# Retention by blocks with a carried state, and four picking rounds moved into the sparse attention

## What is computed

```python
def retention(q, k, v, gate):          # chunks of C = 128 tokens, N = 4 chunks
    scores = einsum('bnchd,bnmhd->bnhcm', qf, kf) * decay_in      # inside a chunk
    inner = einsum('bnhcm,bnmhd->bnchd', scores, vf)
    chunk_state = einsum('bnmhk,hm,bnmhv->bnhkv', kf, zeta, vf)   # K^T V of a chunk
    # scan over chunks: R <- chunk_decay * R + state, prev = R before the chunk
    cross = einsum('bnchk,bnhkv,hc->bnchv', qf, prev, xi)
    o = (inner + cross)
    o = o * rsqrt(mean(o * o, axis=-1) + EPS)                     # per token and head
    return o * silu(gate)

def dsa_attention(q, k, v, qi, ki, wi):  # per block of 128 queries
    iscore = sum_h relu(qi . ki) * wi, causal
    _, sel = top_k(iscore, 128)
    p = softmax(q . k[sel] * d ** -0.5);  out = p @ v[sel]
```

## Time and profile before

| | us |
|---|---|
| median of 3 runs (2241.92 to 2244.69) | 2242.39 |
| the profiled execution | 2242.63 |
| its span on the core | 2240.7 |
| PE busy | 2124.0 (95%) |
| DVE busy | 1257.8 (56%) |
| ACT busy | 806.5 (36%) |
| POOL busy | 78.9 (4%) |

### The profile page before, as it was taken

The page is one execution under the profiler, slowest core; times in us unless marked ns, Lnnn a source line. Parts: engine busy times, 40 slices in busy tenths (PEclk is TensorE's granted clock), DMA queues, the critical chain, the costliest instruction groups (busy, mean ns, idle before and its releaser), DMA issues.

```text
span 2240.7 us, 28429 instructions
## 1 busy us (share of the span) xinstructions
PE 2124.0 (95%) x10880; PEld 1735.8 (77%) x10880; DVE 1257.8 (56%) x2223; ACT 806.5 (36%) x1468; POOL 78.9 (4%) x89
## 2 busy tenths in 40 slices
PE   6998898999999899999999999989879999999998
PEld 5786576888888688887788888778856677888887
DVE  4588447778654424683654545575776746322334
ACT  3333544333423435213422222243446644222222
POOL 0003200000000010000000000001001100000000
PEclk9999798999999899999999999999989999999999
DMA  5221123656442232101355545512400013433221
GB/s 189 89 84 38 38 76 106 204 169 207 132 169 94 74 105 89 44 1 57 123 182 193 176 162 170 169 62 66 151 2 2 2 57 113 132 94 94 94 99 53
DMA packets 146835, 233.10 MB, mean 104 GB/s; under 512 B 7341, under 2 KB 83725, under 8 KB 146445
## 3 DMA queue, kind: packets, MB, share of 16 engines
q1 hardware_dynamic: 144444, 225.81, 30.9%
q0 software_dynamic: 864, 3.15, 0.4%
q10 hardware_dynamic: 1392, 2.33, 0.3%
HBM read 229.16 MB, written 2.10 MB: 103 GB/s over the span
## 4 chain that ended last, share of the span: by engine, by line
PE 80%; DVE 11%; ACT 4%; issue 3%; POOL 1%; DMA 0%; DVEq 0%; POOLq 0%; SPq 0%; ACTq 0%
PE ps L2178 11%; PE ps L2180 11%; PE ps L2179 11%; PE ps L2205 4%; PE ps L2207 4%; PE ps L2206 4%; PE ps L2366 4%; PE ps L2138 4%; PE ps L2139 4%; PE ps L2140 4%; PE ps L2449 4%; PE ps L2368 3%; PE ps L2226 3%; PE ps L2251 2%; PE ps L2238 2%
## 5 line engine op out<-in xcount | busy, mean ns | idle before, releaser
L1543 DVE TENSOR_TENSOR w_lo<-ring,w_hi 128x1024 fp32r<-128x1024 f32 (+4 forms) x362 | 376.4, 1041 | 763.7 <-ACT w_hi L965 763.3
L965 ACT ACTIVATE w_hi<-ring 128x1024 fp32r<-128x1024 f32 (+4 forms) x362 | 329.6, 912 | 975.5 <-PE ps L2180 472.9
L2178 PE MATMUL ps<-x_hi,w_hi 128*128 128x512 f32 x1056 | 416.5, 394 | 0.0
L2180 PE MATMUL ps<-x_hi,w_lo 128*128 128x512 f32 x1056 | 411.2, 389 | 0.0
L2179 PE MATMUL ps<-x_lo,w_hi 128*128 128x512 f32 x1056 | 411.0, 389 | 0.0
L2179 PEld LDWEIGHTS ps<-x_lo,w_hi 128*128 128x128 f32 x1056 | 198.6, 188 | 42.7 <-issue 1.9
L2178 PEld LDWEIGHTS ps<-x_hi,w_hi 128*128 128x128 f32 x1056 | 198.6, 188 | 42.3 <-issue 1.9
L2180 PEld LDWEIGHTS ps<-x_hi,w_lo 128*128 128x128 f32 x1056 | 198.3, 188 | 41.8
L2205 PE MATMUL ps<-w_hi,x_hi 128*128 128x512 f32 x480 | 187.5, 391 | 4.0 <-DVE x_hi L1619 4.0
L2207 PE MATMUL ps<-w_hi,x_hi 128*128 128x512 f32 x480 | 186.8, 389 | 0.0
L2206 PE MATMUL ps<-w_lo,x_hi 128*128 128x512 f32 x480 | 186.8, 389 | 0.0
(11 more groups left out here) (312 smaller groups left out, 3118.3 us busy)
## 6 DMA issues: line engine op xcount, KB each, us to landing
ring<-in_ada_w SPq DMA_DIRECT2D x48, 1024.0 KB, 5.1
ring<-in_ffn_w_in SPq DMA_DIRECT2D x88, 512.0 KB, 4.7
ring<-in_w_up SPq DMA_DIRECT2D x44, 512.0 KB, 4.5
ring<-in_ffn_w_out SPq DMA_DIRECT2D x20, 1024.0 KB, 4.9
ring<-in_hgrn_w_in SPq DMA_DIRECT2D x16, 1024.0 KB, 5.2
ring<-in_w_in SPq DMA_DIRECT2D x12, 1024.0 KB, 5.0
ring<-in_w_down SPq DMA_DIRECT2D x10, 1024.0 KB, 4.9
ring<-in_kv_ada_w SPq DMA_DIRECT2D x8, 1024.0 KB, 5.2
```

What stands on the lines that cost most here:

```text
L965: a.activation(to[:, n % depth, 0:src.shape[-1]], src, ACT.Copy).then_inc(s["hi_done"], 1)
L1543: v.tensor_tensor(to[:, n % depth, 0:width], src, hi[:, n % depth, 0:width].bitcast(F32), ALU.subtract).then_inc(s["lo_done"], 1)
L2178: mm(bs[j], wh[:, k, c], x_hi[:, 2 * q + k], start=first, stop=False)
L2180: ins = mm(bs[j], wl[:, k, c], x_hi[:, 2 * q + k], start=False, stop=last)
```

## The change

Retention is done by blocks with states. The decay of a head is split into a factor of the key's place in its block, which scales rv, and one of the query's place, which scales the output. Of the table of decays (8 times 512 columns, loaded through the weight ring) a table of 664 columns is left, loaded with the constants at the start.

- rv is copied out by ACT in 8 pieces of 128x64 for each of the 4 token tiles, each with its scale.
- PE makes K^T V of three blocks (12 products of 128x128). DVE carries the state on in five tensor operations, which stand behind the fourth of six picking rounds.
- PE makes the scores inside the four blocks only, for two heads at a time in the two halves of the array (8 products of 128x128 for a pair of heads); POOL only masks (one operation a head). The output of a pair of heads takes 14 products of 128x64: two for the first block, four for each other.
- ACT copies the output and its square out. The sums of squares are taken by DVE ahead of unit 8 of the attention, the root by ACT ahead of its unit 10, the scaling by DVE ahead of unit 16.
- Of the ten picking rounds behind P1, four are taken ahead of the units 1, 3, 5 and 7 of the attention, and the picks are made into a bias ahead of unit 8.

```diff
+            pool.wait_ge(s["ret_tab_in"], 16)
             for h in range(RH):
-                for m in range(NT):
...
-                    ins = g.tensor_tensor(sT[:, h % 2, o:o + n], sT[:, h % 2, o:o + n], dec[:, h * S:h * S + n], ALU.mult)
...
+                evacuated(pool, ("ret_s", h))
+                w = ret_sT[:, h % 4].rearrange("p (t n) -> p t n", t=NT)
+                g.tensor_tensor(w, w, ret_causal.unsqueeze(1).broadcast_to([P, NT, P]), ALU.mult).then_inc(s["decayed"], 1)
...
+                if name == "rv":
+                    p = filled(act, (name, t))
+                    act.wait_ge(s["ret_tab_in"], 16)
+                    for h in range(RH):
+                        f = slice(h * HD, (h + 1) * HD)
+                        ins = a.activation(rv_tok[:, t, f], p[:, f], ACT.Identity, scale=ret_key[:, h:h + 1])
+                    ins.then_inc(free((name, t)), 1)
+                    return
...
-            act.wait_ge(s["zero_done"], 2)
-            for t in range(NT):
-                evacuated(act, ("rk", "T", t))
-            a.activation(rk_pair[1][64:128], rk_pair[0][64:128], ACT.Copy).then_inc(s["rk_shifted"], 1)
...
             for t in range(NT):
                 p = filled(act, ("ret_o", t))
-                if t >= 1:
-                    act.wait_ge(s["ret_rms"], t)
-                a.activation(ada_acc[:, 0], p, ACT.Square).then_inc(s["ret_square"], 1)
-            act.wait_ge(s["ret_rms"], NT)
-            a.activation(stat[:, 64:96], stat[:, 32:64], ACT.Sqrt, scale=1.0 / HD, bias=eps[:, :]).then_inc(s["ret_square"], 1)
-            attention("dsa", None)
+                a.activation(mixed[:, t, 0:512], p, ACT.Copy).then_inc(s["ret_square"], 1)
+                a.activation(ret_sq[:, t], p, ACT.Square).then_inc(free(("ret_o", t)), 1)
+
+            def ret_root(i):
+
+                if i == RH + 2:
+                    act.wait_ge(s["ret_rms"], 1)
+                    a.activation(stat[:, 64:96], stat[:, 32:64], ACT.Sqrt, scale=1.0 / HD, bias=eps[:, :]).then_inc(s["ret_square"], 1)
+
+            attention("dsa", ret_root)
...
-            for r in range(EARLY_ROUNDS, TOPK // 8):
+            LATE_ROUNDS = 4
+            for r in range(EARLY_ROUNDS, TOPK // 8 - LATE_ROUNDS):
                 pick_max()
                 pick_replace()
...
+                if r == EARLY_ROUNDS + 3:
+                    dve.wait_ge(s["ret_tab_in"], 16)
+                    for t in range(NT - 1):
+                        p = filled(dve, ("ret_kv", t))
+                        R = ret_R[:, t]
+                        if t == 0:
+                            v.tensor_tensor(R, p, ret_carry, ALU.mult).then_inc(free(("ret_kv", t)), 1)
+                            evacuated(dve, ("ret_kv", t))
+                        else:
+                            v.tensor_tensor(R, p, ret_R[:, t - 1], ALU.add).then_inc(free(("ret_kv", t)), 1)
+                            evacuated(dve, ("ret_kv", t))
+                            v.tensor_tensor(R, R, ret_carry, ALU.mult).then_inc(s["ret_carried"], 1)
+                            dve.wait_ge(s["ret_carried"], t)
...
             def dsa_bias(i):
+                if i < RH and i % 2:
+                    pick_max()
+                    pick_replace()
+                if i == RH:
+                    picks_to_bias()
                 if i % RH == 0 and i // RH >= 1:
                     dve.wait_ge(s["picked"], i // RH)
+                if i == RH:
...
+                        step(v.tensor_reduce(sums[:, t], ret_sq[:, t].rearrange("p (h d) -> p h d", h=RH), AX, ALU.add))
+                    after()
+                    v.tensor_tensor(sums, sums, by_token(ret_query_2), ALU.mult).then_inc(s["ret_rms"], 1)
+                if i == 2 * RH:
+                    dve.wait_ge(s["ret_square"], NT + 1)
+                    step(v.reciprocal(stat[:, 96:128], stat[:, 64:96]))
+                    after()
+                    r = stat[:, 96:128].rearrange("p (t h) -> p t h", t=NT)
+                    step(v.tensor_tensor(r, r, by_token(ret_query), ALU.mult))
+                    after()
+                    for t in range(NT):
+                        w = mixed[:, t, 0:512].rearrange("p (h d) -> p h d", h=RH)
+                        v.tensor_tensor(w, w, bcast(r[:, t].unsqueeze(2), [P, RH, HD]), ALU.mult).then_inc(s["ret_scaled"], 1)
...
-            pe.wait_ge(s["zero_done"], 3)
...
+            for t in range(NT - 1):
+                b = open_bank(("ret_kv", t))
+                for g in range(4):
+                    c = slice(g * P, (g + 1) * P)
+                    ins = mm(b[:, c], rk_tok[:, t, c], rv_tok[:, t, c], start=True, stop=True)
+                ins.then_inc(full(("ret_kv", t)), 1)
...
+            for g in range(RH // 2 + 1):
+                if g < RH // 2:
+                    banks = [open_bank(("ret_s", 2 * g + q)) for q in range(2)]
...
+                            ins = mm(banks[q][:, c], T1["rk"][rows_of(q), g, c], T1["rq"][rows_of(q), g, c], start=True, stop=True)
...
+                if g >= 1:
                     for t in range(NT):
...
+                            if t == 1:
+                                evacuated(pe, ("ret_kv", 0))
+                                pe.wait_ge(s["ret_carried"], 2)
...
+                            if t == 0:
+                                pe.wait_ge(s["decayed"], h + 1)
+                            else:
+                                mm(obs[t][:, f], T1["rq"][:, g - 1, t * P:(t + 1) * P], ret_R[:, t - 1, f], start=True, stop=False)
+                            ins = mm(obs[t][:, f], ret_sT[:, h % 4, t * P:(t + 1) * P], rv_tok[:, t, h * HD:(h + 1) * HD],
+                                     start=(t == 0), stop=True)
```

More of the change, by code:

```diff
@@ L82, in shape_constants @@
     small = np.concatenate([np.eye(P), rope.reshape(P, -1), strip, cmp_bias.reshape(P, -1), (t >= 31) * 1.0], axis=1)
-    return {"c_small": small.astype(f), "c_decay": decay.astype(f).reshape(P, RH * S),
+    return {"c_small": small.astype(f), "c_ret": ret.astype(f),
             "c_masks": np.stack(masks, 1).astype(f)}
@@ L1045, in ffn, with attention @@
                         a.activation(hid_parts(k)[0], hid[:, k], ACT.Copy).then_inc(s["hid_hi"], 1)
-            def attention(name, after_t):
+            def attention(name, between):
                 unit_of, n_units, (L, PB, PT, OT), base = ATT[name]
@@ L1051, in attention @@
                     if i < n_units:
+                        if between:
+                            between(i)
                         u = unit_of(i)
@@ new lines, in picks_to_bias, with by_token @@
+            def picks_to_bias():
+                filled(dve, ("rg", NT - 1))
+                after()
+                for t in range(1, NT):
+                    w = isc[t - 1]
+                    v.tensor_scalar(sel_bias[t - 1], w, REPLACED / 2, NEG, ALU.is_ge, ALU.mult).then_inc(s["picked"], 1)
+            def by_token(w):
+                return bcast(w.unsqueeze(1), [P, NT, RH])
+            def dsa_bias(i):
+                if i < RH and i % 2:
[3 more added lines that the diff above has]
+                    picks_to_bias()
@@ L1775, in dsa_bias @@
                 if i % RH == 0 and i // RH >= 1:
                     dve.wait_ge(s["picked"], i // RH)
+                if i == RH:
+                    sums = stat[:, 32:64].rearrange("p (t h) -> p t h", t=NT)
+                    for t in range(NT):
+                        evacuated(dve, ("ret_o", t))
+                        step(v.tensor_reduce(sums[:, t], ret_sq[:, t].rearrange("p (h d) -> p h d", h=RH), AX, ALU.add))
+                    after()
+                    v.tensor_tensor(sums, sums, by_token(ret_query_2), ALU.mult).then_inc(s["ret_rms"], 1)
@@ new lines, in _ @@
+                        c = slice(m * P, (m + 1) * P)
+                        for q in range(2):
+                            ins = mm(banks[q][:, c], T1["rk"][rows_of(q), g, c], T1["rq"][rows_of(q), g, c], start=True, stop=True)
+                            if m == NT - 1:
+                                ins.then_inc(full(("ret_s", 2 * g + q)), 1)
+                if g >= 1:
+                    for t in range(NT):
+                        if g == 1:
+                            if t == 1:
+                                evacuated(pe, ("ret_kv", 0))
+                                pe.wait_ge(s["ret_carried"], 2)
+                            obs[t] = open_bank(("ret_o", t))
+                        for q in range(2):
+                            h = 2 * g - 2 + q
+                            f = slice(h * HD, (h + 1) * HD)
+                            if t == 0:
[4 more added lines that the diff above has]
+                                     start=(t == 0), stop=True)
+                            if t == NT - 1 and g < RH // 2:
+                                ins.then_inc(s["ret_pv"], 1)
+                        if g == RH // 2:
```

108 lines of the change are left out of this document (33 added, 75 removed).

## The result

The changed kernel took 2254.49 us in the median of 5 runs (2250.4 to 2255.95), against 2242.39 for the kernel before (2241.92 to 2244.69). The ratio is 1.0045, its 95% interval 1.0034 to 1.0056: slower, inside the forecast range and 2.7 us above the forecast. The profiled execution took 2251.66 us, 2.8 less than the median; its span is 2249.9, 9.2 more than before.

A forecast was written before the change was run, and what follows sets the result against it. PE was taken as the bound, busy 95% of the span. Five terms, 2.7 - 12.0 + 14.2 + 3.5 + 1.0 = +9.4 us, on 2242.6 gave 2252.0, as a median 2251.8; range 2240 to 2258.

The forecast's parts named there:

- C: Attention's first block, unit 0 to unit 8: four picking rounds, bias and sums unhidden on DVE, +14.2 us.
- B: From P1's end to the first unit's bias: retention by blocks, its 108 small products at half clock, -12.0 us.
- the fall at 235.5: Granted clock of the kernel before falling to 0.50 behind 128x64 products; taken as evidence against full clock in retention.
- the gap ahead of the products: Behind P1's end, PE nearly idle for 4 us before the 128x64 products, leaving the clock at 0.50.
- My rival: Full clock comes back in retention or never leaves it: 2237.9 to 2240.9 us in total, chance 0.17.
- A: rv scaled by 32 ACT activations before P1's end: relus and index products come later, PE waits, +2.7 us.
- D: Attention's second block, unit 8 to 16: root and table loads on ACT, DVE's reciprocal and products, partly hidden, +3.5 us.
- E: Attention's last two blocks, unit 16 to mix1: extra DVE and ACT work thins PE out, +1.0 us.
- Behind mix1: The program after mix1: nothing edited there, so only the time up to mix1 was priced.

The follow-up runs named there:

- the experiment with early states: Changed kernel with the five operations on the state behind the second picking round in place of the fourth: 2250.33 us, ratio 1.0032.
- The filled kernel: Changed kernel with PE's waits ahead of the first product with a state filled by eight products of 128x384: 2238.34 us, ratio 0.9976.
- the combined kernel: Changed kernel with nine rounds ahead of the attention, earlier state operations, PE fillers, rv scaled by DVE, POOL's gate products held back: 2224.86 us.
- the spread one: The combined kernel with DVE's work for retention's norm spread over the attention's units: 2220.57 us, ratio 0.9897.

## Why the prediction came out as it did

**Sign and size were right; the cause given for one term was only half right.** The change is slower because rounds that DVE did for nothing beside retention now stand in front of the attention's pairs. I had that (C), and undoing it alone brings the stage back to what it took before (199.26 against 199.06).

**B, -13.0 for -12.0.** The items: the states came 10.5 us behind P1's end (10.1 forecast), because the two products that read and write SBUF alone took 0.98 and 0.92 beside POOL; without POOL, in the experiment with early states, all five took 0.69. The 108 instructions were 0.21 apart, as forecast. Each group of scores took 2.08 us at half clock, 0.5 a pair, where I put 0.75 from the attention's first pair; that is 2 us of the gain. What was wrong is the reason that I gave for the half clock: "128x64 products keep PE on the weight load for half their time ... it was under such a run that the clock fell". The filled kernel ran the same products at 1.00 throughout. And the row on which I had leaned, the fall at 235.5 in the kernel before, I read without the wait that stood directly ahead of it:

```profile
234.20 3.41 PE L2333 MATMUL ps<-arena 128*128 128x64 f32 x20 [0.67 <-POOL arena L781]
```

So there too the small products lost the clock behind a wait. The reason that the runs leave is the one I had in the same paragraph beside it, the gap ahead of the products, and of it 2.0 us were enough where I had counted on 4. The rule of the Trainium skill that I had set against it ("TensorE: Matmul & The Clock Gate", Part 1, What's actually happening: idleness throttles, activity releases) is borne out in its first half. In its second it is not here: 22.0 us at 100% busy by the profile, from 212 to 234, released nothing. My rival had the full clock come back in retention or never leave it; in this kernel it did neither, and why 22 us of busy small products don't bring it back stays open. It was within reach all the same: eight added products of 128x384 kept it and brought 13.2 us, so the -25.9 that I had given it for B was sound (-26.2 measured in the filled kernel).

**C, +13.2 for +14.2.** Rounds, waits and sums came as worked out (the four sums 2.46 us); the bias took 0.8 us in place of 1.4.

**A, +4.8 for +2.7, the largest miss.** The activations took 6.67 us (6.7 forecast) and the chain through `high`, `low` and relu was late by what I said. The index products and their waits (1.34 us in all) took 6.4 us (90.40 to 96.80) in place of 3.25, which PE's rows of the kernel before show from the first index product to the next weight piece:

```profile
91.55 3.32 PE L2311 MATMUL ps<-arena 64*128 64x256 f32 x16
...
94.80 0.50 PE L2138 MATMUL ps<-w_hi,x_hi 128*128 128x512 f32 x1
```

What I left out is that these waits take the clock: it was at 0.50 from about 93.6 on, so most of the last eight index instructions ran at half, and so did the next weight piece until 100.4, 3.6 us for what takes 1.8. I had priced the wait and not the clock behind it. DVE's version of the scaling removed all 4.8.

**D, +5.2 for +3.5.** Wrong in its parts: I let 3.5 of the 6.1 us that ACT and DVE got count, and ACT's 2.9 counted nothing; I took DVE's four products at 0.62, and two of them took 1.75 since each released a POOL product that reads and writes SBUF too. The Trainium skill states this ("SBUF — State Buffer", Who interferes with whom): a DVE product with both inputs in SBUF and a GpSimd operation that reads SBUF shut each other out, and the later one waits until the other is through. The trace agrees: 1.75 is 0.62 and the rest of a POOL product of 1.24 (1.1 of it).

**E, +2.5 for +1.0.** The wait of 4.96 ahead of the pair at 272.02 took the clock once more, until about 277. With the wait 2 us shorter E was +1.4.

**Behind mix1, -2.5 for 0.** "Behind mix1 nothing is edited" is true of the instructions, but the time there was not the same. Part of it lies between the same two turns, in the kernel before and then in the changed one:

```profile
1591.50:1608.50 17.00, 13.03 (x90) 0.80 0.10 30
```

```profile
1602.20:1618.00 15.80, 11.81 (x90) 0.89 0.11 34
```

The same 90 instructions take 1.2 us less at a higher granted clock. But this is no effect of the change that the runs show. In the twelve profiles the whole time behind mix1 is 1946.6 to 1950.2 us and doesn't follow the stage: the two extremes are the combined kernel and the spread one built on it, and the changed kernel and the one without the root's table, which agree within 0.2 us in the stage, differ by 0.8 here. Each is one execution. So 2.5 us of the comparison may be nothing but the spread from one execution to the next; what the clock does there was not tried and stays open.

The sum came out near the mark because the misses have both signs: my figures for A, D and E were 5.3 too low in sum, those for B and C 2.0 too high and that for the part behind mix1 2.5 too high, and the first index product came 1.2 sooner. So it is luck that +9.4 stands beside a measured +9.2; against the median the forecast was 2.7 too low.

## What to carry to other kernels

When work is moved from an engine's idle time to an idle time of another stage, ask which engine is waited for there: four rounds of 2.97 us were free beside retention and cost 11.6 us between units whose scores wait for DVE. When a form of the work with smaller products is put behind a wait, price the wait twice, once for itself and once for the clock that the work behind it gets; filling 4.9 us of idle PE was worth 13 us to 108 small instructions and the scores between them, and in the first block of the attention filling cost 2.2 us. And give each released helper (here POOL's gate) a look: started a few us later it takes nothing from the engine on the path.

## What the runs showed of the hardware

- A run of 140 instructions, 108 of them of 128x64 and the rest half-array scores, held the granted clock at 1.00 for 14.5 us, all busy; much the same run did not bring it back in 22.0 us at 0.50, also all busy. Under products of 128x384 it did come back: three of them (six instructions) starting at 218.46 took 3.85 us, the next three 2.20.
- Waits of 1.30 and 0.73 us with short products around them were enough to lose it in retention; in the index products of the changed kernel so were waits of 0.51 and 0.52. The length of the waits alone doesn't tell when it falls: it was still at 1.00 in the first 3.9 us of the wait ahead of 272.02, in the spread kernel from 238 to 242 with PE busy for 2.26 of 4.00 us, and in the kernel with early states behind index waits of 0.49 and 0.52; there it fell with the next one, of 0.83.
- Two scores of 64x128 in different halves of the array, issued as a run of eight pairs, took 0.26 us a pair at full clock (2.06 for 8) and half clock doubled that to 0.5 (2.08 for 4); the lone pair of the attention takes 0.80 at half.
- DVE and POOL products that read two SBUF operands: 0.62 and 1.24 us from one tile of 128x512 to the next alone, 1.75 and about 1.7 beside each other. DVE's addition at 204.50, which reads one operand from PSUM, took 0.69 beside POOL and was not slowed.
- The root starts 0.02 us behind its table load (257.94 behind 256.64 + 1.28), as before.
